# First attention of a two-block network: the scores of both heads of a group in one step, interleaved on the two row halves of TensorE

## What is computed

```python
def forgetting_attention(q, k, v, c):        # B, H=4, S=512, dh=64; block of 128 queries
    s = jnp.einsum("bhqd,bhkd->bhqk", qi.astype(jnp.float32) * scale, kf)
    s = s + ci[..., None] - c[:, :, None, :]
    s = jnp.where(kpos[None, :] <= t[:, None], s, NEG_INF)
    return jnp.einsum("bhqk,bhkd->bhqd", jax.nn.softmax(s, axis=-1), vf)

def dilated_attention(q, k, v):              # the same with three dilated windows, whose
    s = jnp.einsum("bhqd,bhqnd->bhqn", qs, kg)   # weights are summed before the division
```

## Time and profile before

| | us |
|---|---|
| runs of the kernel | 2038.13, 2041.5, 2042.33 |
| median | 2041.5 |
| profiled execution: its span, first to last instruction | 2034.0 |
| PE busy in the span | 1948.5 (96%) |
| VectorE, ScalarE, GpSimd busy | 1070.4, 820.0, 259.3 |
| first attention, from the first score to the output projection | 149.2 to 294.8 |

### The profile page before, as it was taken

The page is one execution under the profiler, slowest core; times in us unless marked ns, Lnnn a source line. Parts: engine busy times, 40 slices in busy tenths (PEclk is TensorE's granted clock), DMA queues, the critical chain, the costliest instruction groups (busy, mean ns, idle before and its releaser), DMA issues.

```text
span 2034.0 us, 25376 instructions
## 1 busy us (share of the span) xinstructions
PE 1948.5 (96%) x8818; PEld 1583.3 (78%) x8818; DVE 1070.4 (53%) x1531; ACT 820.0 (40%) x1216; POOL 259.3 (13%) x206
## 2 busy tenths in 40 slices
PE   6998999989999999999999999999998999999998
PEld 4866778768888878888788888887776578888886
DVE  6665656637767732647644443244676354444323
ACT  4225444425555521553434443134555344444222
POOL 3802122002000000400200000021643020000001
PEclk9996899989999999998999999999997799999999
DMA  4230122112222232221222223232110022222222
GB/s 151 101 104 32 63 76 100 63 42 88 98 93 93 93 114 93 93 92 64 89 87 103 93 93 103 93 109 87 63 62 32 11 93 93 96 100 94 102 93 83
DMA packets 59111, 174.41 MB, mean 86 GB/s; under 512 B 5416, under 2 KB 19880, under 8 KB 58800
## 3 DMA queue, kind: packets, MB, share of 16 engines
q1 hardware_dynamic: 57696, 169.50, 24.9%
q10 hardware_dynamic: 1024, 2.94, 0.4%
q0 software_dynamic: 336, 1.25, 0.2%
HBM read 171.57 MB, written 2.10 MB: 85 GB/s over the span
## 4 chain that ended last, share of the span: by engine, by line
PE 81%; DVE 8%; issue 5%; ACT 4%; POOL 1%; DVEq 0%; DMA 0%; ACTq 0%; POOLq 0%; SPq 0%
PE ps L413 26%; PE ps L415 25%; PE ps L414 25%; ACT w_hi L915 2%; DVE conv_a L1789 1%; DVE conv_g L1789 1%; PE ps L817 1%; DVE w_lo L1407 1%; DVE r_cols L1420 1%; PE ps L879 1%; PE ps L828 1%; POOL square_sum L2066 1%; DVE at_e L1998 1%; PE ps L577 1%; DVE up_g L1428 1%
## 5 line engine op out<-in xcount | busy, mean ns | idle before, releaser
L1407 DVE TENSOR_TENSOR w_lo<-w_raw,w_hi 128x1024 fp32r<-128x1024 f32 x302 | 379.2, 1256 | 508.9 <-ACT w_hi L915 508.6
L413 PE MATMUL ps<-xg_hi,w_hi 128*128 128x512 f32 (+1 forms) x1448 | 568.9, 393 | 28.0 <-DMA con<-in_consts 13.9
L414 PE MATMUL ps<-xg_lo,w_hi 128*128 128x512 f32 (+1 forms) x1448 | 561.3, 388 | 0.0
L415 PE MATMUL ps<-xg_hi,w_lo 128*128 128x512 f32 (+1 forms) x1448 | 561.3, 388 | 0.0
L915 ACT ACTIVATE w_hi<-w_raw 128x1024 fp32r<-128x1024 f32 x302 | 317.7, 1053 | 581.3 <-PE ps L415 577.3
L413 PEld LDWEIGHTS ps<-xg_hi,w_hi 128*128 128x128 f32 x1448 | 275.5, 190 | 98.4 <-DVE w_lo L1407 15.7
L415 PEld LDWEIGHTS ps<-xg_hi,w_lo 128*128 128x128 f32 x1448 | 275.6, 190 | 54.9
L414 PEld LDWEIGHTS ps<-xg_lo,w_hi 128*128 128x128 f32 x1448 | 276.0, 191 | 53.8 <-issue 1.0
L413 PE MATMUL ps<-hid_hi,w_hi 128*128 (+1 forms) x528 | 206.3, 391 | 3.5 <-DVE w_lo L1407 3.5
L415 PE MATMUL ps<-hid_hi,w_lo 128*128 (+1 forms) x528 | 206.1, 390 | 0.0
L414 PE MATMUL ps<-hid_lo,w_hi 128*128 (+1 forms) x528 | 206.0, 390 | 0.0
(11 more groups left out here) (319 smaller groups left out, 2663.5 us busy)
## 6 DMA issues: line engine op xcount, KB each, us to landing
w_raw<-in_weights SPq DMA_DIRECT2D x315, 512.0 KB, 3.2
x<-in_x_cols SPq DMA_DIRECT2D x2, 1024.0 KB, 7.3
out_cols<-result SPq DMA_DIRECT2D x8, 256.0 KB, 2.2
squares<-in_mem_cols ACTq DMA_DIRECT2D x1, 512.0 KB, 3.8
sp_w<-in_spatial ACTq DMA_DIRECT2D x1, 512.0 KB, 3.6
sp_b<-in_spatial_bias ACTq DMA_DIRECT2D x1, 512.0 KB, 4.5
dil<-in_dil_table POOLq DMA_DIRECT2D x1, 448.0 KB, 6.6
alibi<-in_alibi_table ACTq DMA_DIRECT2D x1, 448.0 KB
```

The lines of the kernel that those rows point to most:

```text
L413: nc.tensor.matmul(to, wh, xh, start=start, stop=False)
L414: nc.tensor.matmul(to, wh, xl, start=False, stop=False)
L415: return nc.tensor.matmul(to, wl, xh, start=False, stop=stop)
L1407: nc.vector.tensor_tensor(w_lo[:, u % 2, :], w_raw[:, u % 2, :], w_hi[:, u % 2, :].bitcast(F32), ALU.subtract).then_inc(w_ready, 1)
```

## The change

Scores are issued in even steps only, for items t and t + 1 together: six matmuls, in which the two heads take turns, head 0 on rows 0 to 63 into bank 0 and head 1 on rows 64 to 127 into bank 1. Each head's last matmul adds one to the count of scores. The wait is now for `least(t - 1)`, since both banks are taken over at once. The other engines' programs are the same, in the same order.

```diff
             def scores(t):
-                b, h = t % 8 // 2, t % 2
-                rows = slice(HD * h, HD * h + HD)
+
+                b = t % 8 // 2
                 if t % 8 == 0:
                     pe.wait_ge(a1["staged"], t // 8 + 1)
                 if t >= 2:
-                    pe.wait_ge(a1["least"], t - 1)
+                    pe.wait_ge(a1["least"], t)
                 w = P * (b + 1)
                 qh, ql, kh, kl = group_buffers(t, ("qhi", "qlo", "khi", "klo"))
-                product(ps[:, t % 2, 0:w], qh[rows, b * P:(b + 1) * P], ql[rows, b * P:(b + 1) * P],
-                        kh[rows, 0:w], kl[rows, 0:w], True, True).then_inc(a1["scores"], 1)
+                block_ = slice(b * P, (b + 1) * P)
+                for k, (q_, k_) in enumerate(((qh, kh), (qh, kl), (ql, kh))):
+                    for h in range(2):
+                        rows = slice(HD * h, HD * h + HD)
+                        mm = nc.tensor.matmul(ps[:, h, 0:w], q_[rows, block_], k_[rows, 0:w], start=k == 0, stop=k == 2)
+                        if k == 2:
+                            mm.then_inc(a1["scores"], 1)
...
-                if t < MIX_ITEMS:
+                if t < MIX_ITEMS and t % 2 == 0:
                     scores(t)
```

## The result

The changed kernel takes **2024.0 us** (median of 5 runs, 2021.55 to 2026.65) beside 2038.13 us for the kernel before (5 runs, the three shown earlier among them): ratio 0.9934, interval 0.9918 to 0.995. Taken a second time, the ratio was 0.9926 (0.99 to 0.9953). Two of the later executions of the kernel before, at a granted clock of 0.825 and 0.738, took 2209.45 and 2448.55 us and are in no ratio.

The account below looks back on a forecast made before the run. TensorE (PE), 81% of the chain that ended last, was taken as the bound. Terms in the first attention summed to 10.7 us, taking the median from 2041.5 to 2030.8 us; range 2025.0 to 2036.5 us.

Parts of the forecast that it names:

- The pair: Six score matmuls of two heads in an even step: 0.90 us with 512 keys, second head costed at nothing.
- Odd steps at the full clock: First attention, score removed: 0.66 us gained in each of steps 9, 17, 25 and 0.70 in each of 11, 19, 27.
- Step 3: First attention's opening: last gate product moves up by the score removed before it, gaining 1.0 us.
- Step 23: First attention: gains 0.2 us of 1.07, only the slack until VectorE's split of item 19 is late.
- Steps 15 and 31: First attention, 512-wide scores removed: 2 x 1.07 = 2.1 us at full-clock price, though both lie partly in low clock.
- Hand-overs: Steps 13, 21 and 29, where groups end: no gain, the 0.89 us of each only lengthening PE's idle time.
- the upper end: Largest gain if everything put as hidden shows: 6.1 us more, 16.8 us in all, giving 2024.7 us.
- steps 5 and 7: First attention's opening, scores removed at the low clock where PE ends late: 1.47 + 1.83 = 3.3 us.
- Rival 1: More hidden terms show, perhaps with the opening returning to full clock sooner: 2025 to 2028 us, chance 0.12.
- Rival 3: The halves do not overlap in the first attention, a pair costing two singles: no change, 2042 us, chance 0.05.
- Rivals 2 and 4: First: longer PE idle at hand-overs lowers clock, 2033 to 2037 us, 0.19; second: stage stays low-clocked, 2045.6 us or more, 0.04.
- The base: Whole kernel before: span 2034.0 us, median 2041.5 us, the 7.5 us between them carried to the forecast unchanged.

Follow-up runs that it names:

- before_again: The kernel before, unchanged, profiled and timed once more: ratio 1.0017 to itself.
- after_again: The changed kernel, unchanged, profiled and timed once more: 2021.84 us, ratio 0.9926 to the kernel before.
- serial_heads: The changed kernel with head 0's three score matmuls issued before head 1's, not interleaved: 2021.16 us, ratio 0.9926 to the kernel before.
- single_128: The changed kernel with one head's scores per step in steps 8, 9, 16, 17, 24 and 25 (128 keys): 2022.54 us, one run, no ratio.
- single_at_handover: The changed kernel with items 12, 13, 20, 21, 28 and 29 scored one head per step: 2022.29 us, ratio 0.9926 to the kernel before.
- output_by_head: The changed kernel with each group's output copied and split per head, head 0's one step earlier: 2015.38 us, ratio 0.9889 to the kernel before.
- output_by_head_v_later: As output_by_head, with the next group's values also staged one step later: 2014.27 us, ratio 0.9886 to the kernel before.
- the two half changes: The kernel before with pairs in the first group alone (2030.87 us, ratio 0.9963), or in the other three groups alone (2030.94 us, 0.9965).

## Why the prediction was right in kind and too small

**The pair.** Right: 0.90 us measured, 0.90 forecast.

**Odd steps at the full clock.** Right. Steps 9, 17 and 25 gained 0.67, 0.66 and 0.66 us (forecast 0.66 each); 11, 19 and 27 gained 0.73, 0.73 and 0.75 (0.70). Step 3 gained 0.93 (1.0). Single heads at 128 keys gave steps 9, 17 and 25 back exactly. Step 23 gained 0.26 (0.2), but only in this profile: in the other two of the changed kernel step 22 lies partly at the low clock and takes 4.5 us, VectorE is not late behind it, and step 23 takes 2.38 and 2.39 us for 3.45 and 3.47 before.

**Steps 15 and 31.** Right in sum, though not step by step: the steps that follow a hand-over lie partly at the low clock, so they are counted with the step ahead. Steps 14 and 15 together went from 8.07 to 6.72 us, 30 and 31 from 8.02 to 6.91: 1.35 and 1.11 for 1.07 each. I had not seen that step 15 becomes VectorE-bound (0.96 us before the next turn) where step 14 runs at the high clock; staging the values later gave 0.60 us of it back. In the other two profiles of the changed kernel step 14 takes 4.5 us and there is no such wait, with 6.96 and 6.98 us for both steps.

**Hand-overs.** Right at 13 and 29, which gained nothing, and the unchanged steps with single heads there confirm it. Step 21 gained 0.59 us: in the kernel before it lies at the low clock in all three profiles and took 5.09 for the others' 4.46.

**The step that failed** is the clock that the sum held fixed. Every term was priced at the clock of its place before, so the stage's 52 us at the low clock stayed as they were, and neither the sum nor the upper end (16.8 us) had a term for fewer of them. They fell to 34 to 40 us in three profiles, and the stage gained 13.5 to 14.8 us for 10.7. In the first pair of profiles it shows most in the price of steps 5 and 7 "at the low clock, where PE ends late and the others wait", 1.47 + 1.83 = 3.3 us. It takes the score out and leaves the rest of those steps at the low clock. But steps 5 to 7 went from 19.27 us at 0.59 to 13.34 us at 0.79, 5.9 us. That is 2.6 of the 4.1 us by which the stage's gain exceeds the sum (14.8 - 10.7); 0.6 us is step 21 and 0.5 us step 22, also at another clock. The place is not fixed: in the second profiles of both kernels steps 5 to 7 gained only 2.2 us (14.83 to 12.63), while steps 22, 23 and 28 to 31, lower in clock in that profile of the kernel before, gained 2.4 us more than in the first. Steps 5 to 7 in `before_again`, then in `after_again`:

```profile
166.32:181.15 14.83, 12.30 (x71) 0.84 0.11 36
165.69:178.32 12.63, 10.10 (x68) 0.85 0.10 31
```

The timeline shows what differs. PE in the second half of step 6 in the first profile of the kernel before, behind its wait for ScalarE:

```profile
178.69 0.55 PE L413 MATMUL ps<-xg_hi,w_hi 128*128 128x256 f32 x1 [2.55 <-ACT mem_rms_rows L1093]
179.04 0.42 PE L414 MATMUL ps<-xg_lo,w_hi 128*128 128x256 f32 x1
179.26 0.42 PE L415 MATMUL ps<-xg_hi,w_lo 128*128 128x256 f32 x1
```

and in the changed kernel:

```profile
173.48 0.36 PE L413 MATMUL ps<-xg_hi,w_hi 128*128 128x256 f32 x1 [2.54 <-ACT mem_rms_rows L1098]
173.68 0.28 PE L414 MATMUL ps<-xg_lo,w_hi 128*128 128x256 f32 x1
173.79 0.28 PE L415 MATMUL ps<-xg_hi,w_lo 128*128 128x256 f32 x1
```

The wait is the same; behind it the last two of these matmuls start 0.22 us apart before and 0.11 us after. Rival 1 had said this ("the opening returns to full clock sooner") and I gave it 0.12, because VectorE's and ScalarE's chains stood against the rest of it. Those chains held; the clock moved. In the first profiles the low-clock time fell from 2 x 0.18 x 145.6 = 52 us to 2 x 0.13 x 130.76 = 34 us; at the 0.43 at most per microsecond that the prediction used, up to 7.9 us, of which about 4 appeared. Rival 3 falls with the pair of 0.90 us.

Rivals 2 and 4 had the longer idle time at the hand-overs cost clock. Their outcome did not come: the wait there grew from 0.46 to 1.36 us, and the stage's clock rose. But their mechanism is not refuted. Behind step 7 the stage has a clock of 0.92, 0.86 and 0.92 in the three profiles before and of 0.95, 0.92 and 0.93 in those of the changed kernel, and it is higher in the three paired kernels that shorten the waits again, at the first hand-over from 1.36 + 0.74 us to about 1.2. (`serial_heads` and `single_128`, with the changed kernel's waits, have 0.95 and 0.93. The kernel before also waits 1.2 us there, so the wait alone does not set the clock.) From the start of step 8, the changed kernel, `single_at_handover`, `output_by_head` and `output_by_head_v_later`:

```profile
179.21:278.03 98.82, 88.89 (x613) 0.95 0.23 77
181.15:279.16 98.01, 90.10 (x612) 0.97 0.25 80
180.69:274.55 93.86, 85.35 (x611) 0.98 0.25 84
179.60:270.76 91.16, 83.83 (x613) 1.00 0.24 83
```

So some low-clock time may well have been left by those waits, as rival 2 had it, inside a stage whose clock rose on the whole. There is one profile of each of these kernels, so this is argued and not shown.

**The base.** The 7.5 us between the span and the median were carried "unchanged". In the two later profiles of the kernel before the execution's own time lies 1.8 us above its span (2036.0 for 2034.2, 2038.31 for 2036.5), and the kernel before has a median of 2038.13 us over five runs and 2036.85 over 23. Of the 6.8 us by which 2030.8 was too high, 2041.5 - 2038.13 = 3.4 us are the base, and 3.4 us the gain (14.1 measured between medians, 10.7 forecast). It took both to leave the range: with the base of five runs it would have begun at 2021.6 us, below the 2024.0 measured, and with the gain as forecast the time would have been 2027.4 us.

**What stays open.** That the clock's rise comes with the pairs is shown by three profiles of each kernel and by the two half changes. Why PE is granted it is not shown: the pairs bring fewer changes of form, shorter odd steps and longer waits at once, and the kernels that change the hand-over's waits alone or nearly so have one profile each.

## What to carry to other kernels

Read the price of a removed instruction from the step in which it stands, and then ask who is late next: here that gave the terms to within 0.1 us at full clock, nothing at the hand-overs, and the next two changes worth making. Where a stage lies partly at the low clock, its clock is part of what the change moves; put the low-clock time of the whole stage into the range on both sides, not on the losing side alone, and compare such stages by their totals and over more than one profile, since the low clock falls on other steps in another execution. And a median of three carried from another execution can be off: here by 3.4 us, a quarter of the gain.

## What the hardware showed that was not expected

Matmuls on the two row halves run beside each other whatever their order: with all three matmuls of head 0 ahead of head 1's the pair took 0.90 us, as it did interleaved, and as long as one head alone (0.89 us). And the granted clock of the stage rose from 0.81 or 0.82 to between 0.85 and 0.87 although PE's busy share there fell (134.27 of 145.60 us, 114.15 of 130.76 now) and its single waits at the hand-overs grew; where those were shortened afterwards, it rose again, to 0.89 to 0.91.
